# Pairwise norm by tile on GpSimd, heads ahead of weight splits, and two MLP units by token in a two-layer transformer kernel

## The reference

```
h_x = modulate(rms_norm(x, norm_g[l, 0]), sh1_x, sc1_x)
m_x, m_c = even_mixer(...)  # layer 0: heads A (grouped) and B (differential)
m_x, m_c = odd_mixer(...)   # layer 1: heads C (window, sink) and D (neighborhood)
x = x + g1_x * rms_norm(m_x, norm_g[l, 1])
f_x = squared_relu_mlp(modulate(rms_norm(x, norm_g[l, 2]), sh2_x, sc2_x), w_mlp_in[l], w_mlp_out[l])
x = x + g2_x * rms_norm(f_x, norm_g[l, 3])

o_b = (rms_norm(o_b, subln_g) * (1 - lam0)).reshape(B, T, -1)     # even_mixer, each pair of heads
qc, kc = apply_axial_rope(qc, cos, sin), apply_axial_rope(kc, cos, sin)   # odd_mixer
jnp.square(jax.nn.relu(h @ w1)) @ w2                              # squared_relu_mlp
```

## Time and profile before

| | us |
|---|---|
| median of 3 runs | 1590.78 |
| lowest, highest | 1589.05, 1591.47 |
| the profiled execution | 1591.33 |
| its span in the trace | 1589.4 |

### The profile page before, as it was taken

One profiled execution on the slowest core, in us unless ns is written; L12 is line 12 of the kernel. 1 busy time (PEld: TensorE's weight loads), 2 busy tenths in 40 slices (PEclk: granted clock), 3 DMA queues, 4 the chain that ended last, 5 costly groups with the idle time before them and its releaser, 6 DMA issues.

```text
span 1589.4 us, 24201 instructions
## 1 busy us (share of the span) xinstructions
PE 1524.4 (96%) x9562; PEld 1304.0 (82%) x9562; DVE 859.9 (54%) x1472; ACT 677.3 (43%) x1096; POOL 172.6 (11%) x165
## 2 busy tenths in 40 slices
PE   9999899999999989999799999999998999889998
PEld 7998698999996865786689777777787887779997
DVE  5786655554545864347465443433447546655444
ACT  5454344545445334426454222231225446544443
POOL 3100220000000110000414001110002020021110
PEclk9999999999999989999899999999999999989999
DMA  6456565453436315211213443544512421235451
GB/s 253 176 188 228 214 223 182 162 199 134 164 128 239 136 63 203 107 53 54 80 59 127 160 185 133 212 163 155 212 54 90 142 75 54 92 147 203 168 199 67
DMA packets 43769, 233.81 MB, mean 147 GB/s; under 512 B 13264, under 2 KB 14224, under 8 KB 16784
## 3 DMA queue, kind: packets, MB, share of 16 engines
...
## 4 chain that ended last, share of the span: by engine, by line
PE 45%; DVE 3%; POOL 1%; ACT 1%; issue 1%; DVEq 0%; ACTq 0%
PE ps L552 13%; PE ps L554 13%; PE ps L553 13%; PE ps L764 2%; PE ps L650 1%; DVE wlo L1044 1%; PE ps L702 1%; PE ps L736 1%; POOL flo L2281 1%; ACT whi L1034 0%; PE ps L612 0%; PE ps L634 0%; POOL mix L2319 0%; ACT fhi L1093 0%; DVE mix L1969 0%
## 5 line engine op out<-in xcount | busy, mean ns | idle before, releaser
L1044 DVE TENSOR_TENSOR wlo<-raw,whi 128x2048 fp32r<-128x2048 f32 x162 | 381.5, 2380 | 250.6 <-ACT whi L1034 250.3
L552 PE MATMUL ps<-fhi,whi 128*128 128x256 f32 (+1 forms) x1280 | 391.2, 306 | 9.4 <-DVE wlo L1044 3.9
L1034 ACT ACTIVATE whi<-raw 128x2048 fp32r<-128x2048 f32 x162 | 304.5, 1906 | 211.8 <-PE ps L554 162.9
L554 PE MATMUL ps<-fhi,wlo 128*128 128x256 f32 (+1 forms) x1280 | 387.3, 303 | 0.0
L553 PE MATMUL ps<-flo,whi 128*128 128x256 f32 (+1 forms) x1280 | 387.2, 302 | 0.0
L552 PEld LDWEIGHTS ps<-fhi,whi 128*128 128x128 f32 x1280 | 245.9, 192 | 33.0 <-issue 9.5
L553 PEld LDWEIGHTS ps<-flo,whi 128*128 128x128 f32 x1280 | 246.0, 192 | 8.8
L554 PEld LDWEIGHTS ps<-fhi,wlo 128*128 128x128 f32 x1280 | 245.8, 192 | 8.9
L552 PE MATMUL ps<-whi,fhi 128*128 128x512 f32 (+1 forms) x592 | 209.1, 353 | 9.7 <-DVE e_b L2116 4.5
L553 PE MATMUL ps<-wlo,fhi 128*128 128x512 f32 (+1 forms) x592 | 205.3, 347 | 0.0
L554 PE MATMUL ps<-whi,flo 128*128 128x512 f32 (+1 forms) x592 | 205.2, 347 | 0.0
...
## 6 DMA issues: line engine op xcount, KB each, us to landing
raw<-in_wstream SPq DMA_DIRECT2D x210, 1024.0 KB, 5.0
...
```

The lines of the kernel that those rows point to most:

```text
L552: mm(o, lh, rh, start=start, stop=False)
L554: return mm(o, ll, rh, start=False, stop=stop)
L1034: nc.scalar.activation(whi[:, w % SPLIT_SLOTS, :], raw[:, c % RAW_SLOTS, :], ACT.Copy).then_inc(*did("scalar", ("hi", w)))
L1044: nc.vector.tensor_tensor(wlo[:, w % SPLIT_SLOTS, :], raw[:, c % RAW_SLOTS, :], whi[:, w % SPLIT_SLOTS, :].bitcast(F32), ALU.subtract).the ...
```

## The change

Four edits, and what belongs to them.

1. *Pair norm by tile.* VectorE's guess and GpSimd's Newton steps and scalings run once per tile, on four columns, in the order 2, 3, 0, 1. The turns of the mixed rows of tiles 2 and 3 move from items 15 and 16 to items 16 and 17.
2. *Heads ahead of splits.* In layer 1 VectorE rotates both query tiles and key tile 0 before it splits any chunk of the next unit; ScalarE's three copies of chunks stand one by one between the copies of values and heads; TensorE turns each query tile behind a key tile; `mod_columns(1, 1)` goes ahead of the modulation.
3. *MLP units 0 and 1 of layer 1 by token.* Features are turned, modulated and halved tile by tile in layout 128x4x128, the hidden values come out token by channel, are squared in one piece of 128x512, turned back by TensorE (`turn_hidden`) and halved by ScalarE and VectorE. The tile turns and hidden turns stand inside other units (`between`). Units 2 to 7 stay as they are.
4. *Column halves.* `mlp_out` waits for the chunk of the column half that it is about to use, in both layers. And `table_for(ACT.Sqrt)` does a square root of one column that nobody reads, ahead of the splits of `out2`.

```
-            return ([(1, ("v2", 0, 1, 0)), (3, ("v2", 0, 1, 1))] + [(15 + j // 2, ("fo", j)) for j in range(4)]
+            return ([(1, ("v2", 0, 1, 0)), (3, ("v2", 0, 1, 1))] + [(16 + j // 2, ("fo", j)) for j in range(4)]
...
             def wait_feature(name, k):
-                if k % 2 == 0:
-                    pe.wait_ge(*after("split", name, k // 2))
-            def by_token(u, name, tiles, kt=KD, width=NW, feat=None, first=True, last=True, side=0):
+                step = 4 if name[0] == "n2 tile" else 2
+                if k % step == 0:
+                    pe.wait_ge(*after("split", name, k // step))
+            def by_token(u, name, tiles, kt=KD, width=NW, feat=None, first=True, last=True, side=0,
+                         between=()):
...
+                        for at, turns_now in between:
+                            if at == k:
+                                turns_now()
...
+            def turn_tile(t):
+                pe.wait_ge(*after("xn", 1, 1, t))
+                for j in range(2):
+                    o = job("n2 tile", t, j)
+                    for q in range(4):
+                        k = 4 * j + q
+                        ins = nc.tensor.transpose(o[:, q * P:(q + 1) * P], mix[:, t, k * P:k * P + P], ident[:, :])
+                    ins.then_inc(*did("tensor", ("n2 tile", t, j)))
+            def turn_hidden(j, t):
+                o = job("hidden turn", j, t)
+                pe.wait_ge(*after("squared tile", j, t))
+                for e in range(4):
+                    ins = nc.tensor.transpose(o[:, e * P:(e + 1) * P], htmp[:, j, e * P:e * P + P], ident[:, :])
+                ins.then_inc(*did("tensor", ("hidden turn", j, t)))
...
                 u = UNIT["out", l, i]
                 if first:
-                    for k in (0, 4):
-                        wait_weights(u, k)
                     for e in range(4):
-                        pe.wait_ge(*after("hidden", l, i, e))
+                        if not l or i >= 2:
+                            pe.wait_ge(*after("hidden", l, i, e))
+                        elif e < 2:
+                            pe.wait_ge(*after("hidden", "tile", i, e))
                 b = i % 2
                 for n in ns:
+                    wait_weights(u, u.nk * n)
...
-                        by_token(u, ("k2", l, 0), (2, 3), width=256, feat=("n1", l, 1), first=False)
-                        turn_heads("q", 0, range(nt), 4)
+                        by_token(u, ("k2", l, 0), [2], width=256, feat=("n1", l, 1), first=False, last=False)
+                        turn_heads("q", 0, [0], 4)
+                        by_token(u, ("k2", l, 0), [3], width=256, first=False)
+                        turn_heads("q", 0, [1], 4)
...
-                        by_token(UNIT["out2", 1, n], ("out2", 1, n), [t], feat=None if n or t else ("fo", 1, 0),
-                                 first=t == 0, last=t == 1)
-                turn_normed(1, 1, 0)
+                        by_token(UNIT["out2", 1, n], ("out2", 1, n), [t], feat=None if n or t else ("fo", 1, 0), first=t == 0,
+                                 last=t == 1, between=[(3, lambda: turn_tile(0))] if t and n else [])
+                by_token(UNIT["in", 1, 0], ("in tile", 0), [0], feat=("n2 tile", 0), last=False)
+                by_token(UNIT["in", 1, 1], ("in tile", 1), [0], last=False,
+                         between=[(4, lambda: turn_tile(1)), (6, lambda: turn_hidden(0, 0))])
+                by_token(UNIT["in", 1, 0], ("in tile", 0), [1], feat=("n2 tile", 1), first=False,
+                         between=[(5, lambda: turn_hidden(1, 0))])
+                by_token(UNIT["in", 1, 1], ("in tile", 1), [1], first=False, between=[(5, lambda: turn_hidden(0, 1))])
                 for t in range(XT):
                     for n in range(2):
                         held[t, n] = job("acc", t, n)
                 state["banks"] = [b for b in range(8) if b not in [counts.banks[("acc", t, n)] for t in range(2) for n in range(2)]]
-                for j in range(9):
-                    if j < 8:
-                        by_feature(UNIT[("in", l, j)], ("in", l, j), 0, nt * P, feat=None if j else ("n2", l, 0))
-                    if 0 < j < 8:
-                        mlp_out(l, j - 1, range(nt))
+                mlp_out(1, 0, range(2), ns=(0,), last=False)
+                turn_hidden(1, 1)
+                mlp_out(1, 0, range(2), ns=(1,), first=False)
+                for j in range(2, 8):
+                    by_feature(UNIT["in", 1, j], ("in", 1, j), 0, S)
+                    mlp_out(1, j - 1, range(2))
...
+                        ahead = PLACE[UNIT["q2", 1, 1].w0]
+                        for t in (0, 1):
+                            values_part(t)
+                        split_hi(act, ahead, st)
+                        values_part(2)
+                        turned("q", 0, 0)
+                        split_hi(act, ahead + 1, st)
+                        values_part(3)
+                        turned("q", 0, 1)
+                        for t in range(4):
+                            turned("k", 0, t)
+                        split_hi(act, ahead + 2, st)
...
+                table_for(ACT.Sqrt)
                 split_to(("out2", 1, 0))
                 for n in range(2):
                     half_square(1, 0, 0, n)
...
                 stream_root(1, 1, (0,))
                 half_square(1, 0, 1, 0)
                 split_to(("out2", 1, 1))
+                tile_features(0)
                 half_square(1, 0, 1, 1)
                 mixer_root(1, 0, (1,))
+                split_hi(act, PLACE[UNIT["in", 1, 1].w0], st)
                 stream_root(1, 1, (1,))
+                split_to(("in", 1, 1), 0)
                 load_gates(l, 1)
-                split_features(("n2", 1, 0), 0, (1, 1))
-                for j in range(9):
-                    if j < 8:
-                        split_to(("in", l, j))
-                        hidden(l, j)
-                    if j:
-                        split_to(("out", l, j - 1))
+                relu_tile(0, 0)
+                tile_features(1)
+                high_tile(0, 0)
+                relu_tile(1, 0)
+                high_tile(1, 0)
+                relu_tile(0, 1)
+                split_hi(act, PLACE[UNIT["out", 1, 0].w0], st)
+                high_tile(0, 1)
+                split_to(("out", 1, 0), 0)
+                relu_tile(1, 1)
+                high_tile(1, 1)
...
+                    ahead = PLACE[UNIT["q2", 1, 1].w0]
+                    dve.wait_ge(loads["odd"], 48)
+                    for t in (0, 1):
+                        stage("q", 1, 0, t)
+                    stage("k", 1, 0, 0)
+                    split_lo(ahead, st)
+                    for t in (1, 2, 3):
+                        stage("k", 1, 0, t)
+                    link(v.tensor_scalar(nsink[:, :], sinkr[:, :], -1.0, None, ALU.mult))
+                    split_lo(ahead + 2, st)
+                    gate_rows(1)
...
+                modulate_tile(0)
+                split_to(("in", 1, 0), 0)
                 sum_halves(1, 0, (1,))
                 gated_half(1, 0, 1, 1)
                 residual(1, 0, (1,))
+                split_lo(PLACE[UNIT["in", 1, 1].w0], st)
                 normed(1, 1, (1,))
-                modulate(("n2", 1, 0), 1, 1, 0)
-                for j in range(9):
-                    if j < 8:
-                        split_to(("in", l, j))
-                        square_hidden(l, j)
-                    if j:
-                        split_to(("out", l, j - 1))
+                split_to(("in", 1, 1), 0)
+                square_tile(0, 0)
+                modulate_tile(1)
+                low_tile(0, 0)
+                square_tile(1, 0)
+                low_tile(1, 0)
+                square_tile(0, 1)
+                split_lo(PLACE[UNIT["out", 1, 0].w0], st)
+                low_tile(0, 1)
+                split_to(("out", 1, 0), 0)
+                square_tile(1, 1)
+                low_tile(1, 1)
...
-            for t in (3, 1):
-                pair_norm((t - 1, t))
+            for t in (2, 3, 0, 1):
+                pair_norm(t)
```

140 lines of the change are left out of this document (92 added, 48 removed).

## The result

| | before | changed |
|---|---|---|
| median of the runs, us | 1590.03 (1589.05 to 1591.47) | 1578.09 (1574.28 to 1579.03) |
| ratio, with its 95% interval | | 0.992 (0.9901 to 0.9939) |
| profiled execution, us | 1591.33 | 1574.28 |
| its span, us, and mean granted clock | 1589.4, 0.983 | 1572.3, 0.992 |

The change is worth 12 us, not the 22.6 of the prediction, and 1578.09 lies outside the range of 1564.5 to 1575.5. The profiled execution of the changed kernel is the quickest of its four. It is 17.05 us ahead of the profiled one of before, where the medians are 11.9 apart: its mean granted clock is 0.992, that of its three other runs 0.988 to 0.989. 3.1 of the 17.05 arise ahead of stretch A, where no instruction is new. The clock bears on these too: up to there TensorE is busy for 716.0 us at 0.98 before and for 713.5 at 0.99 in the changed kernel.

The account below looks back on a forecast made before the run. TensorE's own work plus its holes was taken to bound the kernel. A 7.0, B 7.3 and C 8.3 sum to 22.6 us, taking the profiled 1591.33 us to a forecast median of 1568.0 us; range 1564.5 to 1575.5 us.

Parts of the forecast that it names:

- stretch A: End of layer 0's attention: TensorE's waits for pair norm shrink, gaining 7.0 us, bounds 4.3 to 8.4.
- C: From layer 1's mixer into its MLP: unit 2 starts earlier, gaining 8.3 us, bounds 4.5 to 13.9.
- A, first hole: TensorE's 4.27 us wait for GpSimd's scaling of tiles 2 and 3: gone, with its 1.5 us lower-clock echo.
- A, second hole: TensorE's 3.50 us wait for pair norm of tiles 0 and 1: some 2.3 us stays.
- the queue of tile 0: End of layer 0's attention: tile 0's norm, newly in GpSimd's queue, meets the weight splits and adds 1.3 us.
- B: Rotation of heads in layer 1: TensorE's 4.54 us wait goes, first scores 7.3 us earlier, bounds 4.5 to 7.8.
- (3): Layer 1's MLP unit 0, tile 0: starts at 1390.2, waits 0.7 us for the second low half, through at 1396.3.
- (5): Layer 1's MLP units 0 and 1: token order takes 21.8 us plus 1.8 of transposes; waits 0.2 and 0.5 us.
- (6): Layer 1's MLP: waits by column half let the first out unit start at 1417.1 and unit 2 at 1428.5.
- GpSimd stays behind both splits: Rival in C and A: TensorE loses 2.2 us in C, up to 1.5 in A; 1572 us, chance 0.17.
- The token order passes the wait on: Rival in C: VectorE's queue sets the pace, unit 2 starts at 1433; 1575 us, chance 0.13.
- Slower: Rival from layer 1's unit 2 on: late splits lag through six units, costing 27 us; 1595 us, chance 0.02.

Follow-up runs that it names:

- alone: The kernel before with only heads rotated ahead of the splits in the last layer, no new tile: 1583.49 us, ratio 0.9959.

## Why the prediction missed

**The three terms were right to within 1.5 us each; a fourth was missing.** In place of 22.6: 6.6 + 7.35 + 6.8 from the traces, less some 8 us for the operands' place. With the tile taken out the time is 1569.73, where 1568.0 was forecast. The step that failed is "In layer 0 the separate wait for column halves meets no hole, nor do the units behind C: nothing". For the wait it holds, but the sentence stood for everything outside the stretches, and I had costed the first line of the diff, a tile of 4 bytes per partition that moves the operands of 1344 matmuls, nowhere. In its place the runs show 6.2 ns for each of these matmuls, 8.3 us. None of the rivals had it either, so the range could not: its lower bounds came from the same three stretches. (Its upper sum takes 10.7 us for C, a figure that is worked out nowhere in the prediction; the miss is at the other end.)

**A, first hole** (4.3 us and its echo of 1.5). Gone. TensorE even came to the second turns at 775.4 in the old clock (776.59 less 4.25, plus 3.1), not at 776.9.

**A, second hole.** Forecast: turns at 779.2, wait 2.3. Measured: 779.7 in the old clock, wait 4.25. The time at which GpSimd was done was sized well (1.3 us for the queue of tile 0; it was about 1.7). The wait is 2 us longer than forecast, 1.5 of it because TensorE was earlier and 0.5 because GpSimd was later, and the term came out at 6.6 for 7.0. By its own words "one wait of about 2 us" was wrong: I read a wait off two forecasts and their errors added.

**B.** 7.35 for 7.3; alone 7.0. First scores at 1237.1 forecast, at 1237.07 in the old clock (1231.92 + 5.15).

**C.** Changed kernel, timeline of TensorE, answering to the earlier trace rows; and its busy time in one stretch (PE, PEld, DVE, ACT, POOL, granted clock, DMA).

```profile
1358.41 0.47 PE L553 MATMUL ps<-whi,fhi 128*128 128x512 f32 x1 [0.66 <-DVE wlo L1079]
...
1371.51 1.09 PE L896 MATMUL ps<-ident,mix 128*128 128x128 f32 x8
...
1378.13 0.61 PE L553 MATMUL ps<-whi,fhi 128*128 128x512 f32 x1 [2.10 <-DVE wlo L1079]
...
1386.75 0.47 PE L553 MATMUL ps<-whi,fhi 128*128 128x512 f32 x1 [1.30 <-DVE dev L1710]
...
1394.50 0.47 PE L553 MATMUL ps<-whi,fhi 128*128 128x512 f32 x1 [0.51 <-POOL flo L2494]
...
1406.42 0.40 PE L553 MATMUL ps<-whi,hhi 128*128 128x512 f32 x1
...
1418.05 0.28 PE L553 MATMUL ps<-fhi,whi 128*128 128x256 f32 x1
```

```profile
1376.00:1386.00 10.00, 7.35 (x25) 5.56 (x24) 9.76 (x11) 4.44 (x8) 3.17 (x1) 0.83 0.58 211
```

Add 12.57 for the old clock.

| step | forecast | measured |
|---|---|---|
| (1) wait behind the early table | 0.65 | 0.66 |
| (2) turns of tile 0, no wait | 1383.9 | 1384.1, none |
| (2) through the out projection | 1388.2 | 1388.6 |
| (3) unit 0 starts; wait | 1390.2; 2.0 | 1390.7; 2.10 |
| (3) unit 0, tile 0, with 0.7 for the second low half | 6.1 | 7.3, none of it that wait |
| (4) wait for the split of unit 1 | 1.5 | 1.30 |
| (5) small waits | 0.2, 0.5 | 0.51 |
| (6) first `out` unit | 1417.1 | 1419.0 |
| (6) unit 2 | 1428.5, or 1429.1 with the clock | 1430.6 |

What was mis-sized is the clock, not a wait: behind the 2.1 us hole nine matmuls come 0.43 us apart and not 0.23 (1378.13 to 1381.9), 1.8 us where I had allowed 0.6. With 0.3 us for the first `out` unit's stationary operands, that is the 1.5 us between 1430.6 and 1429.1; the other steps are off by up to 0.5 and cancel.

**The rivals.** "GpSimd stays behind both splits": in A yes, one product waited for both, and the queue of tile 0 cost 0.4 us more than the 1.3 reckoned, not up to 1.5 more. In C of the changed kernel's trace no, its first low half got its turn first and its second between the splits; in two other kernels' traces yes. The mechanism is real, its price of 2.2 us in C was wrong, and its chance of 0.17 was put on a race that fell one way in some traces and the other way in others. "The token order passes the wait on": no, unit 2 came at 1430.6 and not at 1433. "Slower": no wait in units 2 to 7; they come 22.69 us apart against 22.42, all of it in their `out` halves. The last shows how my own test could mislead: "if units 2 to 7 show any wait" looked for waits, and the loss was in the matmuls. "Unit 2 starts 152 us before the end of the span, as now" did catch it: it is 154.25 (1572.3 less 1418.05).
